# Sums of squares of the norms: VectorE folds three of four pairs of blocks before TensorE adds over features

## The chip, the cores and the metric

The kernel runs on one core of a Trainium2 chip. The metric is the device time of one execution in microseconds (us), lower is better. Five engines work side by side: PE (TensorE), DVE (VectorE), ACT (ScalarE), POOL (GpSimd) and SP (SyncE, which here issues the weight transfers). Semaphores alone tie them together.

## The reference

Two transformer blocks of depth 2 each, on one sequence of 256 tokens and 1024 features, in float32. What matters here are the norms over all 1024 features:

```python
def rms_norm(x, g):
    x32 = x.astype(jnp.float32)
    y = x32 * lax.rsqrt(jnp.mean(x32 * x32, axis=-1, keepdims=True) + EPS)
    return (y * g.astype(jnp.float32)).astype(x.dtype)
...
    for l in range(DEPTH):
        h = rms_norm(x, norm_mix_pre[l])
        proj = h @ w_in[l]
...
        x = x + rms_norm(merged @ w_out[l], norm_mix_post[l])

        h2 = rms_norm(x, norm_ffn_pre[l])
        gu = h2 @ w_ffn_in[l]
        f_g, f_u = jnp.split(gu, 2, axis=-1)
        f = (jax.nn.silu(f_g) * f_u) @ w_ffn_out[l]
        x = x + rms_norm(f, norm_ffn_post[l])
```

The second block has such a norm ahead of each of its six stages (mix, memory attention, feed-forward, and in the second layer a mixture of experts), and none behind them: the product is added to `x` as it is.

## The kernel before, in words

Everything lies with features on the 128 partitions and the 256 tokens along the free dimension. `x` is the tile `X`, eight feature blocks of 128 x 256, and is handled in four pairs of blocks (128 x 512), numbered 0 to 3. The program is ten stages in a row: mix and feed-forward of layer 0, the same of layer 1, then mix, memory and feed-forward of the second block, then mix, memory and experts. Each engine's program is one list of steps made in the same order (`steps`), and each engine picks its own kinds out of it, so an engine never passes a step of its own that still waits.

A product with a weight is made of three matmuls on a high and a low part of each operand (L1844, L1845, L1846; `wh` and `wl` are the parts of a weight unit of 128 x 1024). SP loads a unit, ACT copies its high part (L2315), DVE subtracts it for the low part (L2633). There are four slots for split units, so ACT starts the next unit when PE has freed a slot, and DVE follows ACT.

The sum of squares over 1024 features goes as follows. ACT squares a pair of blocks into one of six scratch tiles of `SC` (step `square`, L2330, or inside `y_out`, L2350). The step `sums` has PE multiply each 128 x 128 quarter of it, as the stationary operand, with a column of ones: four matmuls of one column per pair (L1849, written `ps<-CST,SC 128x1`), all 16 of a norm added up in one PSUM bank. The step `mean` has DVE make the inverse root of it in nine small instructions (L2642 and on, tile `RS`), and `spread` has PE copy it over the partitions (128x128 matmuls at L1849).

There are fourteen such norms of eight blocks: ten of `x` (one ahead of each stage; `x_sums`) and four of a stage's result (`ys`, in the mix and feed-forward stages of the first block). They differ in where the sums stand in the order:

- **Result norms** (four): `y_out` gives a square per pair, and the sums of pair n-1 are queued after pair n's product. The last two pairs come together behind the last product, in `residual_rms`, which then waits for the norm and adds it to `x`.
- **Heads** (five: the start of the program and behind each `residual_rms`): the next stage starts with `start`, in which PE multiplies the raw, not yet normed `x` with the first weights in parts of the features (`Wide.part`). Sums of pairs 0 and 1 stand behind the features of pairs 0 and 1, those of pairs 2 and 3 behind the features of pair 2, then `mean`, then the last part.
- **Added stages** (five: behind the stages of the second block): `added` (and a loop like it in `block2_mem`) takes each pair when the product is added to `X` (L2645 `X<-ps,X`), makes its parts (`x_parts` on ACT, L2335, and `x_low` on DVE, L2645 `b<-X,VEC,b`) and its square, and queues the sums of the pair before it. At most the last two pairs are left for `start`.

Two smaller norms (`mean_rs` over four blocks, or over the memory) use the same steps.

Of the kernel before, what the change touches and what calls it, by code (L numbers as in the profile page):

```python
# [175 lines left out]
def build(nc, ctx, ins, out):  # L176
# [205 lines left out]

    def sums(src, nt):
        o = Step("sums")
        o.src, o.nt, o.bk, o.wait, o.end = src, nt, a_bank(full=False), [], None
        return o

    def sums_pe(o, keep=0):
        while len(o.wait) > keep:
            sq = o.wait.pop(0)  # L390
            st = step("sums")
            st.o, st.sq = o, sq
            o.end = st.done = P.next("sums")
            sq.sc.out = st.done

# [7 lines left out]
    def mean_rs(src, nt, scale, eps, rdy, final=1.0, o=None):  # L403
        if o is None:
            o = sums(src, nt)
            for t0 in range(0, nt, 2):
                sums_pair(o, t0, rdy[t0 // 2] if nt == 8 and len(rdy) == 4 else rdy, keep=2)
                if t0 % 4 == 2 or t0 + 2 >= nt:
                    yield
                    sums_pe(o)  # L410
        sums_pe(o)
        st = mean(o, scale, eps, final)
        yield
        return spread(st)
# [645 lines left out]
    def added(g, keep=1):  # L1060

        for _ in g:
            while after:
                p = after.pop(0)
                xp = x_parts(p)
                x_squares(p)
                if p:
                    sums_pe(x_sums[0], keep)
                x_low(xp)
            yield  # L1070
# [768 lines left out]
    def pe_program(e):  # L1839
# [41 lines left out]
        def sums_step(st):  # L1881
# [4 lines left out]
            for u in range(2):  # L1886
                for b in range(2):
                    r = mm(o.bk.ps[:, b:b + 1], v[:, u, b * 128:(b + 1) * 128], ONES[:, 0:1], sq.t0 + u + b == 0, sq.t0 + u + b == o.nt)
            r.then_inc(st.done[0])
# [733 lines left out]
    def dve_program(e):  # L2623
# [54 lines left out]
        def split_step(st):  # L2678
# [4 lines left out]
            else:  # L2683
                stt(st.dst[1], st.src, st.fac, st.dst[0].bitcast(F32), MUL, SUB).then_inc(st.lo[0])

        def mean(st):
            o = st.o
# [635 lines left out]
        def tile_down(st):  # L3323
            if st.ending:
                for m, b in enumerate(st.bks):
# [6 lines left out]
                     up_gate=up_gate, up_gate_w=up_gate, up_rs=up_rs,  # L3332
                     mean=mean, hrs=hrs, scaled=scaled, residual=residual, kr_rope=kr_rope, glu=glu, conv=conv,
                     conv_mean=conv_mean, conv_z=conv_z, conv_y=conv_y, q_turn=q_turn, scores=scores, scores_pen=scores_pen, att_out=att_out, times=times,
# [233 lines left out]
```

## Time and profile before

| | us |
|---|---|
| median of 3 runs | 2828.19 |
| the runs | 2828.08, 2832.55, 2828.19 |
| the profiled execution's own time | 2826.45 |
| span of its instructions | 2824.7 |
| PE busy in the span | 2603.9 (92%) |
| DVE busy | 1949.6 (69%) |
| ACT busy | 1285.6 (46%) |

Mean granted TensorE clock 0.952. Times in the trace count from the first instruction. A matmul of the program in float32 leaves two records in the trace: `128x1 x8` of the program reads x16 there.

### The profile page before, as it was taken

To read this page: it belongs to the slowest core of one execution; us is meant where nothing else is said; L and a number is where in the kernel's file an instruction comes from. 1 tells how busy PE (TensorE), PEld (TensorE's weight loads), DVE (VectorE), ACT (ScalarE), POOL (GpSimd) and SP (SyncE) were. 2 spreads that over 40 slices of the span, in tenths; PEclk is the share of its full clock that TensorE was granted. 3 is DMA by queue.
4 is the path that set the end of the run, shared out by engine and by line. 5 is a ranking of instruction groups with operands and counts; after the bars stand their busy time and mean duration, and the time that the engine had idled before them with its cause. 6 is when DMAs were issued, how large, how long until landed. Compare 5 with 4: busy or idle time off the path is not lost.

```text
span 2824.7 us, 52188 instructions
## 1 busy us (share of the span) xinstructions
PE 2603.9 (92%) x20994; PEld 2423.6 (86%) x20994; DVE 1949.6 (69%) x3287; ACT 1285.6 (46%) x1939; POOL 350.5 (12%) x292
## 2 busy tenths in 40 slices
PE   7979889998799899899989999899888899999999
PEld 7879889988799899888878899888777888888887
DVE  5888767568887675676665676757565557566688
ACT  4445344444453444443333444343333447464576
POOL 0000000000000000000000000000000246455486
PEclk9999999999999999998989999989899799999999
DMA  5444445544444355342024355432032357576687
GB/s 197 155 142 150 142 134 182 181 162 153 140 147 150 130 185 179 122 142 76 18 75 150 120 186 177 156 120 76 17 103 95 131 180 251 199 234 223 199 304 263
DMA packets 135614, 433.90 MB, mean 154 GB/s; under 512 B 15408, under 2 KB 26032, under 8 KB 135120
## 3 DMA queue, kind: packets, MB, share of 16 engines
q1 hardware_dynamic: 94912, 286.25, 30.6%
q0 software_dynamic: 36512, 140.53, 14.7%
q10 hardware_dynamic: 3952, 3.79, 0.5%
q8 instruction: 169, 2.77, 0.4%
q14 instruction: 69, 0.57, 0.1%
HBM read 429.46 MB, written 1.05 MB: 152 GB/s over the span
## 4 chain that ended last, share of the span: by engine, by line
PE 73%; DVE 16%; ACT 5%; issue 4%; DMA 1%; POOL 0%; DVEq 0%; ACTq 0%; POOLq 0%
PE ps L1844 21%; PE ps L1846 20%; PE ps L1845 20%; PE ps L1849 12%; DVE wl L2633 4%; DVE b L2637 3%; DVE b L2645 2%; ACT wh L2315 2%; DVE SC L2645 1%; PE ps L1852 1%; DVE SC L2637 1%; DVE X L2637 0%; ACT SC L2394 0%; ACT b L2325 0%; DVE SC L2641 0%
## 5 line engine op out<-in xcount | busy, mean ns | idle before, releaser
L2633 DVE TENSOR_TENSOR wl<-wf,wh 128x1024 fp32r<-128x1024 f32 (+2 forms) x620 | 729.2, 1204 | 251.6 <-ACT wh L2315 246.8
L1844 PE MATMUL ps<-b,wh 128*128 128x256 f32 x2832 | 819.9, 289 | 89.6 <-DVE wl L2633 38.8
L1845 PE MATMUL ps<-b,wh 128*128 128x256 f32 x2832 | 807.4, 285 | 0.0
L1846 PE MATMUL ps<-b,wl 128*128 128x256 f32 x2832 | 806.1, 285 | 0.0
L2315 ACT ACTIVATE wh<-wf 128x1024 fp32r<-128x1024 f32 (+2 forms) x620 | 625.2, 1038 | 259.6 <-PE ps L1846 227.2
L1844 PEld LDWEIGHTS ps<-b,wh 128*128 128x128 f32 x2832 | 549.6, 194 | 101.2 <-issue 73.5
L1845 PEld LDWEIGHTS ps<-b,wh 128*128 128x128 f32 x2832 | 550.2, 194 | 0.2
L1846 PEld LDWEIGHTS ps<-b,wl 128*128 128x128 f32 x2832 | 549.2, 194 | 0.0
L1844 PE MATMUL ps<-HH,wh 128*128 128x256 f32 x1264 | 376.1, 298 | 37.9 <-DVE wl L2633 37.8
L1845 PE MATMUL ps<-HL,wh 128*128 128x256 f32 x1264 | 363.7, 288 | 0.0
L1846 PE MATMUL ps<-HH,wl 128*128 128x256 f32 x1264 | 363.4, 287 | 0.0
L1844 PEld LDWEIGHTS ps<-HH,wh 128*128 128x128 f32 x1264 | 248.7, 197 | 52.1 <-issue 50.9
L1845 PEld LDWEIGHTS ps<-HL,wh 128*128 128x128 f32 x1264 | 248.8, 197 | 1.9 <-issue 1.4
L1846 PEld LDWEIGHTS ps<-HH,wl 128*128 128x128 f32 x1264 | 248.5, 197 | 0.0
L1844 PE MATMUL ps<-wh,b 128*128 128x512 f32 (+2 forms) x560 | 218.1, 389 | 2.1 <-DVE wl L2633 1.3
L1845 PE MATMUL ps<-wl,b 128*128 128x512 f32 (+2 forms) x560 | 215.2, 384 | 0.0
L1846 PE MATMUL ps<-wh,b 128*128 128x512 f32 (+2 forms) x560 | 215.0, 384 | 0.0
L1849 PE MATMUL ps<-b,b 64*64 64x64 f32 (+5 forms) x3183 | 182.5, 250 | 25.6 <-DVE b L2637 13.4
L1849 PEld LDWEIGHTS ps<-b,b 64*64 64x64 f32 (+2 forms) x3183 | 161.8, 152 | 44.6 <-issue 16.1
L1849 PEld LDWEIGHTS ps<-CST,SC 128*128 128x128 f32 (+2 forms) x1140 | 130.5, 191 | 42.9 <-ACT SC L2363 19.0
L1849 PE MATMUL ps<-CST,SC 128*128 128x1 f32 (+4 forms) x1140 | 135.5, 270 | 33.4 <-DVE SC L2645 16.7
L2633 DVE TENSOR_TENSOR wl<-b,wh 128x1024 fp32r<-128x1024 f32 (+1 forms) x112 | 126.0, 1154 | 29.8 <-ACT wh L2315 29.3
(224 smaller groups left out, 3481.2 us busy)
## 6 DMA issues: line engine op xcount, KB each, us to landing
wf<-in_w_in_b SPq DMA_DIRECT2D x112, 512.0 KB, 4.1
wf<-in_w_in SPq DMA_DIRECT2D x80, 512.0 KB, 3.8
wf<-in_w_ffn_g SPq DMA_DIRECT2D x44, 512.0 KB, 3.5
wf<-in_w_ffn_u SPq DMA_DIRECT2D x44, 512.0 KB, 4.5
wf<-in_w_out SPq DMA_DIRECT2D x32, 512.0 KB, 3.5
wf<-in_w_ffn_out SPq DMA_DIRECT2D x32, 448.0 KB, 4.0
wf<-in_ffn_wg SPq DMA_DIRECT2D x22, 512.0 KB, 3.5
wf<-in_ffn_wu SPq DMA_DIRECT2D x22, 512.0 KB, 4.4
```

Source lines behind the costliest of these rows:

```text
L1844: e.matmul(o, stat[0], mov[0], start=first, stop=False)
L1845: e.matmul(o, stat[0], mov[1], start=False, stop=False)
L1846: return e.matmul(o, stat[1], mov[0], start=False, stop=end)
L1849: return e.matmul(o, l, r, start=first, stop=end)
L1852: return e.transpose(o, l, IDENT[0:l.shape[0], 0:l.shape[0]])
L2315: e.activation(u.whi, u.buf, ACT.Copy).then_inc(u.hi[0])
L2633: e.tensor_tensor(u.wlo, u.buf, u.whi.bitcast(F32), SUB).then_inc(u.lo[0])
L2637: return e.tensor_tensor(o, a, b, op)
L2645: return e.scalar_tensor_tensor(out=o, in0=a, scalar=s, in1=b, op0=op0, op1=op1)
```

## The change

The sums of pairs are no longer all made on PE. The first pair's square tile becomes a total; a new step `fold` has DVE add the squares of pair 1 and then of pair 2 to it in place (128 x 512 each). When pair 3 is taken, PE gets two steps one behind the other: the total, and pair 3. `mean_rs` keeps the old way. In `added` the step `x_low` moves ahead of the sums. ACT's program does not change.

```diff
+    def sums_part(o, sq, first, last):
+        st = step("sums")
+        st.o, st.sq, st.first, st.last = o, sq, first, last
+        o.end = st.done = P.next("sums")
+        sq.sc.out = st.done
 
     def sums_pe(o, keep=0):
         while len(o.wait) > keep:
             sq = o.wait.pop(0)
-            st = step("sums")
-            st.o, st.sq = o, sq
-            o.end = st.done = P.next("sums")
-            sq.sc.out = st.done
+            n = o.seen
+            o.seen += 1
+            if not o.fold:
+                sums_part(o, sq, n == 0, n == o.nt // 2 - 1)
+            elif n == 0:
+                o.total = sq
+            elif n < 3:
+                st = step("fold")
+                st.sc, st.sq, st.before = o.total.sc, sq, o.total.done
+                st.done = sq.sc.out = P.next("fold")
+                o.total = st
+            else:
+                sums_part(o, o.total, True, False)
+                sums_part(o, sq, False, True)
...
                 xp = x_parts(p)
                 x_squares(p)
+                x_low(xp)
                 if p:
                     sums_pe(x_sums[0], keep)
-                x_low(xp)
             yield
...
+        def fold(st):
+            E.wait_ge(st.before)
+            E.wait_ge(st.sq.done)
+            tt(st.sc.v, st.sc.v, st.sq.sc.v, ADD).then_inc(st.done[0])
```

PE, in the head of the first feed-forward stage (behind the features of pair 1; `b_13312` and `b_15360` are the high and low part of x). Before:

```order
L1844 MATMUL ps<-b_13312_128,wh 128x256
L1845 MATMUL ps<-b_15360_129,wh 128x256
L1846 MATMUL ps<-b_13312_128,wl 128x256
L1849 MATMUL ps<-CST,SC 128x1 x8
L1844 MATMUL ps<-b_13312_128,wh 128x256
```

The change, at the same products:

```order
L1861 MATMUL ps<-b_13312_128,wh 128x256
L1862 MATMUL ps<-b_15360_129,wh 128x256
L1863 MATMUL ps<-b_13312_128,wl 128x256
L1861 MATMUL ps<-b_13312_128,wh 128x256
L1862 MATMUL ps<-b_15360_129,wh 128x256
```

The eight sums of pairs 0 and 1 are gone, and the eight behind the features of pair 2 stay, now of the total and pair 3. (All lines behind the diff's first edit move by 17.)

DVE, at the end of the first mix stage: the last splits of weights, then the inverse root of the result norm. Before:

```order
L2645 SCALAR_TENSOR_TENSOR SC<-b_0_106,ps 128x512
L2637 TENSOR_TENSOR b_11264_130<-b_11264_130,SC 128x512
L2637 TENSOR_TENSOR b_15360_132<-b_11264_130,b_13312_131 128x512
L2633 TENSOR_TENSOR wl<-wf,wh 128x1024 x9
L2642 TENSOR_SCALAR RS<-ps 128x2
L2642 TENSOR_SCALAR RS<-RS 128x2
```

The change:

```order
L2654 TENSOR_TENSOR b_15360_132<-b_11264_130,b_13312_131 128x512
L2650 TENSOR_TENSOR wl<-wf,wh 128x1024 x6
L2654 TENSOR_TENSOR SC<-SC 128x512
L2650 TENSOR_TENSOR wl<-wf,wh 128x1024 x3
L2654 TENSOR_TENSOR SC<-SC 128x512
L2659 TENSOR_SCALAR RS<-ps 128x2
```

One fold stands between the splits and the second behind the last of them. In the head that follows, both folds stand behind the last split, right ahead of the inverse root.

DVE, at the end of the second block's first memory stage (`X<-ps,X` adds a pair; `b_15360_228` is the low part of the new x). Before:

```order
L2645 SCALAR_TENSOR_TENSOR X<-ps,X 128x512
L2645 SCALAR_TENSOR_TENSOR b_15360_228<-X,VEC,b_13312_227 128x256 x2
L2633 TENSOR_TENSOR wl<-wf,wh 128x1024 x2
L2645 SCALAR_TENSOR_TENSOR X<-ps,X 128x512
L2645 SCALAR_TENSOR_TENSOR b_15360_228<-X,VEC,b_13312_227 128x256 x2
L2633 TENSOR_TENSOR wl<-wf,wh 128x1024
L2642 TENSOR_SCALAR RS<-ps 128x2
```

The change:

```order
L2662 SCALAR_TENSOR_TENSOR X<-ps,X 128x512
L2662 SCALAR_TENSOR_TENSOR b_15360_228<-X,VEC,b_13312_227 128x256 x2
L2654 TENSOR_TENSOR SC<-SC 128x512
L2650 TENSOR_TENSOR wl<-wf,wh 128x1024 x2
L2662 SCALAR_TENSOR_TENSOR X<-ps,X 128x512
L2662 SCALAR_TENSOR_TENSOR b_15360_228<-X,VEC,b_13312_227 128x256 x2
L2654 TENSOR_TENSOR SC<-SC 128x512
L2650 TENSOR_TENSOR wl<-wf,wh 128x1024
L2659 TENSOR_SCALAR RS<-ps 128x2
```

Each fold stands between a pair's low part and the next split of weights.

## Rows read from the trace of the kernel before

**Rows 1.** The page: busy time, and the chain that ended last.

```profile
PE 2603.9 (92%) x20994; PEld 2423.6 (86%) x20994; DVE 1949.6 (69%) x3287; ACT 1285.6 (46%) x1939; POOL 350.5 (12%) x292
...
PE 73%; DVE 16%; ACT 5%; issue 4%; DMA 1%; POOL 0%; DVEq 0%; ACTq 0%; POOLq 0%
```

**Rows 2.** Timeline of PE: start, us, what; eight sums in a head.

```profile
386.03 1.84 PE L1849 MATMUL ps<-CST,SC 128*128 128x1 f32 x16
...
387.73 0.36 PE L1844 MATMUL ps<-b,wh 128*128 128x256 f32 x1
387.94 0.28 PE L1845 MATMUL ps<-b,wh 128*128 128x256 f32 x1
388.05 0.28 PE L1846 MATMUL ps<-b,wl 128*128 128x256 f32 x1
```

**Rows 3.** Timeline of PE: four sums behind a product of the first feed-forward.

```profile
542.93 0.95 PE L1849 MATMUL ps<-CST,SC 128*128 128x1 f32 x8
543.74 0.36 PE L1844 MATMUL ps<-b,wh 128*128 128x256 f32 x1
```

**Rows 4.** Groups of instructions by form, DVE: nearest form to a fold.

```profile
L2637 DVE TENSOR_TENSOR X<-X,SC 128x512 f32<-128x512 f32 x16 | 11.1, 692 | 0.6
```

**Rows 5.** Timeline of DVE, the same head; idle before and releaser in brackets.

```profile
392.56 0.16 DVE L2642 TENSOR_SCALAR RS<-ps 128x2 f32<-128x2 f32 x1 [8.15 <-PE ps L1849]
```

**Rows 6.** Timeline, end of the first mix stage: PE, then DVE.

```profile
355.58 1.05 PE L1849 MATMUL ps<-CST,SC 128*128 128x1 f32 x8 [0.54 <-ACT SC L2350]
356.50 0.37 PE L1844 MATMUL ps<-b,wh 128*128 128x256 f32 x1
...
368.68 1.90 PE L1849 MATMUL ps<-CST,SC 128*128 128x1 f32 x16
...
354.13 2.36 DVE L2633 TENSOR_TENSOR wl<-wf,wh 128x1024 fp32r<-128x1024 f32 x2 [6.89 <-ACT wh L2315]
...
367.24 1.23 DVE L2633 TENSOR_TENSOR wl<-wf,wh 128x1024 fp32r<-128x1024 f32 x1 [0.18 <-ACT wh L2315]
```

**Rows 7.** Timeline, end of the first feed-forward: PE, DVE, ACT.

```profile
575.66 1.98 PE L1849 MATMUL ps<-CST,SC 128*128 128x1 f32 x16
...
574.56 1.23 DVE L2633 TENSOR_TENSOR wl<-wf,wh 128x1024 fp32r<-128x1024 f32 x1 [1.57 <-ACT wh L2315]
...
575.94 0.60 ACT L2350 ACTIVATE SC<-ps 128x512 f32<-128x512 f32 x1 [1.41 <-PE ps L1846]
```

**Rows 8.** Timeline of PE and DVE: splits of weights that PE waits for.

```profile
1505.27 2.36 DVE L2633 TENSOR_TENSOR wl<-wf,wh 128x1024 fp32r<-128x1024 f32 x2 [0.98 <-ACT wh L2315]
...
1118.40 0.55 PE L1844 MATMUL ps<-b,wh 128*128 128x256 f32 x1 [2.99 <-DVE wl L2633]
...
1589.98 0.36 PE L1844 MATMUL ps<-b,wh 128*128 128x256 f32 x1 [0.19 <-DVE wl L2633]
...
2146.01 0.55 PE L1844 MATMUL ps<-HH,wh 128*128 128x256 f32 x1 [2.99 <-DVE wl L2633]
```

**Rows 9.** Timeline of DVE, end of the first memory stage.

```profile
1575.81 0.68 DVE L2645 SCALAR_TENSOR_TENSOR X<-ps,X 128x512 f32<-128x512 f32 x1
...
1580.08 0.68 DVE L2645 SCALAR_TENSOR_TENSOR X<-ps,X 128x512 f32<-128x512 f32 x1
...
1583.20 2.36 DVE L2633 TENSOR_TENSOR wl<-wf,wh 128x1024 fp32r<-128x1024 f32 x2 [0.98 <-ACT wh L2315]
1585.48 0.68 DVE L2645 SCALAR_TENSOR_TENSOR X<-ps,X 128x512 f32<-128x512 f32 x1
...
1588.61 1.23 DVE L2633 TENSOR_TENSOR wl<-wf,wh 128x1024 fp32r<-128x1024 f32 x1 [0.99 <-ACT wh L2315]
```

**Rows 10.** Timeline of PE: the last four sums, ahead of the experts.

```profile
2219.72 1.03 PE L1849 MATMUL ps<-CST,SC 128*128 128x1 f32 x8
```

**Rows 11.** Stretches: busy us of PE, PEld, DVE, ACT, POOL; granted clock; DMA.

```profile
1118.40:1121.70 3.30, 3.30 (x15) 3.30 (x16) 2.99 (x3) 1.36 (x2) 0.00 (x0) 0.50 0.72 196
...
1738.00:1792.00 54.00, 54.00 (x462) 53.85 (x461) 27.59 (x40) 20.83 (x27) 0.12 (x1) 1.00 0.51 164
```

More of the change, by code:

```diff
@@ L381, in split, with sums @@
         return [st.hi, st.lo]
-    def sums(src, nt):
+    def sums(src, nt, fold=True):
         o = Step("sums")
         o.src, o.nt, o.bk, o.wait, o.end = src, nt, a_bank(full=False), [], None
+        o.seen, o.total, o.fold = 0, None, fold
         return o
+    def sums_part(o, sq, first, last):
[3 more added lines that the diff above has]
+        sq.sc.out = st.done
     def sums_pe(o, keep=0):
@@ L404, in mean_rs @@
         if o is None:
-            o = sums(src, nt)
+            o = sums(src, nt, False)
             for t0 in range(0, nt, 2):
@@ L1887, in sums_step @@
                 for b in range(2):
-                    r = mm(o.bk.ps[:, b:b + 1], v[:, u, b * 128:(b + 1) * 128], ONES[:, 0:1], sq.t0 + u + b == 0, sq.t0 + u + b == o.nt)
+                    r = mm(o.bk.ps[:, b:b + 1], v[:, u, b * 128:(b + 1) * 128], ONES[:, 0:1], st.first and u + b == 0, st.last and u + b == 2)
             r.then_inc(st.done[0])
@@ L3332, in dve_program @@
                      up_gate=up_gate, up_gate_w=up_gate, up_rs=up_rs,
-                     mean=mean, hrs=hrs, scaled=scaled, residual=residual, kr_rope=kr_rope, glu=glu, conv=conv,
+                     fold=fold, mean=mean, hrs=hrs, scaled=scaled, residual=residual, kr_rope=kr_rope, glu=glu, conv=conv,
                      conv_mean=conv_mean, conv_z=conv_z, conv_y=conv_y, q_turn=q_turn, scores=scores, scores_pen=scores_pen, att_out=att_out, times=times,
```

## The prediction

> **What bounds the kernel now.** I began with the page. PE is busy for 2603.9 of 2824.7 us and holds 73% of the chain of work that ended last, DVE is busy for 1949.6 us and holds 16% [rows 1]. So work taken from PE is worth its time where PE runs without a pause, and work given to DVE is free where DVE waits for PE. That is a question for each of the fourteen norms, and the timeline around each answers it. I then read, place by place, when PE starts the sums, what it runs next, where it waits and for whom, and when DVE is free there.
>
> **The price of a sum.** In the head of the first feed-forward the eight matmuls of a group (16 records) start at 386.03 and the next product at 387.73: 1.70 us, 0.106 us a record [rows 2]. The first product behind them also takes 0.21 to the next start (387.73 to 387.94) where the next takes 0.11 (to 388.05), so leaving such a group saves about 0.08 more: 1.78 for eight, and with 0.81 for four (542.93 to 543.74) [rows 3] 0.89 for four.
>
> A rule speaks against this price. The Trainium skill, "TensorE: Matmul & The Clock Gate", section "Back-to-back issue gap", says that matmuls of few columns are bounded by an issue floor of about 25 ns. The 224 records removed would by that be worth an estimated 5.6 us and the time would be about 2823. The rows have 106 ns a record, four times the floor, and the same page's section on LDWEIGHTS gives the reason, an estimated 107 ns for 128 columns of a stationary operand: a sum with one column moves nothing, but loads 128 columns of squares. The trace decides, and I price by it.
>
> **The price of a fold.** No fold is in the trace. The nearest rows are adds of two SBUF tiles of 128 x 512 in float32, 0.692 us each over 16 instructions, in place as the fold is [rows 4]. I take 0.69. The 28 folds make 19.4 us of DVE time at most, and nothing at least.
>
> **Five heads.** DVE waits 8.15 us for PE, from the end of its last split at 384.41 to the inverse root at 392.56 [rows 5]. The squares are done by then, so both folds (1.4 us) are ready at about 385.8, more than 3 us before PE can reach the total. PE loses one group of eight: 1.78 us, and all that follows starts from the sums' end. If DVE's pause were not there the folds would cost 1.4. 5 x 1.78 = **8.9 us**.
>
> **Two mix results.** Ahead of the first product of pair 2 PE waits 0.54 us for the square of pair 0, then does the four sums, and starts the product at 356.50. Without them it could start at 355.0 or a little before, but its weight's low part is ready only at about 355.4 (the first of the two splits that start at 354.13) [rows 6]. So 1.1 is saved, and 0.89 at the next group. At the end the second fold stands behind the last split, which ends at 368.47 (367.24 + 1.23), 0.2 before PE's sums begin at 368.68 [rows 6]. Its high part comes from ACT, which makes a square and its copies just before and moves up only by the first saving and a part of the second, so the split then ends with PE's last product, and PE's lead of 1.99 shrinks by 0.1 and by the fold's 0.73. Net 1.1 us each: **2.2 us**.
>
> **Two feed-forward results.** Two groups of four go. Behind the last product DVE's last split ends at 575.79, so the second fold ends at 576.5. Before, PE did the sums of pair 2 from 575.66 on, while ACT made the last square (575.94 to 576.54) [rows 7]; now it waits for the fold and does all eight after it, 0.81 later. In layer 0 this leaves 2 x 0.89 - 0.81 = 0.97. In layer 1 the first group's gain vanishes, since PE waits 2.99 us for a split a little later, behind the rope tables, whose chain starts from the product and not from the sums [rows 8]. That leaves 0.08. Together **1.05 us**.
>
> **Five added stages.** Before, four sums after pairs 0, 1 and 2, and four (or eight) in the head. Here the last group grows from four to eight where three groups went.
> - First mix stage of the second block (sums of pair 3 already came with pair 2's): the first group's gain falls to a wait for a split that ends at 1506.5, and the second holds: 0.89 [rows 8].
> - First memory stage: DVE and ACT drive it. Add (0.68), parts, square, high part, low part, next add go round in 4.3 to 5.4 us whatever PE does, and the split that PE needs last ends at 1589.84, where PE already waits for it [rows 8, 9]. All three groups' gain is lost, and the final group, now eight, costs 0.81 on the path. The folds themselves fit: 0.69 in the 0.98 that DVE waits between a low part and a split; without that pause each would cost 0.69. Net -0.81.
> - Feed-forward: PE runs without a pause, 54.00 of 54.00 us [rows 11]; 3 x 0.89 - 0.81 = 1.86.
> - Second mix stage: both gains end in the wait of 2.99 at 2146.01, behind a transfer issued when x is ready [rows 8], and x is made by the DVE and ACT loop: 0.
> - Second memory stage: three groups of four go from a PE that runs nearly through, the last, which stood at 2219.72 right ahead of the inverse root, grows and waits a little for a fold behind pair 3's add [rows 10]: about 0.6, chosen between -0.8 and 1.9.
>
> Together **2.5 us**. The moved `x_low` costs nothing: it only keeps the fold out from ahead of a low part.
>
> **Sum.** 8.9 + 2.2 + 1.05 + 2.5 = 14.7 us. From the profiled execution's own 2826.45 that gives 2811.8. The three runs shown have a median 1.7 higher, 2828.19, and against it I predict **2813.5**.
>
> **The rivals.**
> - *Everything PE drops counts.* Of the 112 matmuls, five groups of eight at 1.78 and eighteen of four at 0.89 make 24.9 us: 2803.3. For it: PE's 92%. Against it: the waits just listed. Chance 0.06.
> - *The mixing stages swallow their share.* Long stretches behind the heads of the mix stages run through DVE and ACT chains. If these, and not the sums' end, set the next stage's start, only the two feed-forward heads (3.6) and the feed-forward results (1.05) keep their gain: -4.6, 2823.6, within the bound of 0.2%. Against it: each such chain begins with the inverse root, which waited for the sums [rows 5]. Chance 0.14.
> - *The loads of squares are hidden.* If a sum held PE for next to nothing beside the products, no place would gain, and the new waits for folds would stay, 0.73 behind each mix result and 0.81 behind each feed-forward result: +3.1, 2831.3, also within 0.2%. The page's issue floor is a rule of this kind. Against it: the next product starts 1.70 us later, not at once [rows 2]. Chance 0.03.
> - *The clock turns it into a loss.* Behind a wait of 2.99 us the granted clock is 0.50 for the next stretch (1.2 in place of 2.4 GHz) [rows 8, 11]. There 15 product records fill 3.3 us, 0.22 each; at 54.00 us for 462 records, 0.117 each, they would take 1.8, so that stretch gives away about 1.5 us. The change adds waits of PE: under 1 us behind four result norms, and two of 1 to 2 us in the first memory stage. If each of the fourteen norms brought one more such stretch, 14 x 1.5 = 21 us would go, and the time would be 2834.5. It decides from ten such stretches (no gain left), and can be told from fourteen. Against it: most places get denser, not looser. Chance 0.07.
>
> **How the numbers follow.** What I forecast has 0.70: gains of 9 to 20 us, 2808 to 2819, since how each stretch of low clock falls against the shifted work moves the sum by some microseconds. 0.2% of the time, 5.7 us, is about what can be told from no change. Faster then has 0.70 + 0.06 = 0.76, the same 0.14 + 0.03 = 0.17, slower 0.07. The range leaves out the loss and the outer part of the full gain and takes in the second rival: 2806 to 2825.
>
> **What would show it.** The page after has 224 fewer PE records and 28 more of DVE, the folds as `SC<-SC` of 128 x 512 at 0.69. In the heads PE goes through the features of pair 2 with no sums ahead, and DVE's wait before the inverse root shrinks from 8.15 to about 5. Behind the feed-forward results PE has a new wait of about 0.8 for `DVE SC`. In the first memory stage PE waits longer for splits and the end comes 0.8 later. The forecast is wrong if the folds take much longer than 0.69, if low splits or DVE loops move later by them, or if the mean granted clock falls clearly below 0.952.

## The result, and the profile after

| | before | changed |
|---|---|---|
| median, us | 2828.14 (4 runs) | 2805.15 (4 runs) |
| the runs, us | 2825.18 to 2832.55 | 2801.92, 2802.37, 2807.93, 2808.29 |
| profiled execution, us | 2826.45 | 2801.92 |
| span, us; mean granted clock | 2824.7; 0.952 | 2800.1; 0.955 |

The ratio is 0.9916, with a 95% interval from 0.9904 to 0.9929: 23 us faster. I had predicted 2813.5, 14.7 us faster, with a range down to 2806. The sign was right; the size lies just outside. Two later measurements of the same kernel, below, gave 0.9936 and 0.9945, which is about 2810 and 2813 us when put against the same 2828.14.

The page of the changed kernel, its head and the busy times:

```profile
span 2800.1 us, 51799 instructions
...
PE 2573.4 (92%) x20770; PEld 2394.1 (85%) x20770; DVE 1967.8 (70%) x3315; ACT 1284.7 (46%) x1939; POOL 348.6 (12%) x292
```

Against [rows 1] PE has 224 records fewer and DVE 28 instructions more, and PE's busy time fell by 30.5 us where DVE's grew by 18.2. In the groups of instructions by form, DVE, the folds have a row of their own:

```profile
L2654 DVE TENSOR_TENSOR SC<-SC 128x512 f32<-128x512 f32 x28 | 19.2, 686 | 0.2
```

686 ns each, against the 692 of [rows 4] by which I priced them, and DVE waited 0.2 us for them in all.

The head of the first feed-forward, timeline of PE, then of DVE (start, us, what, in brackets the idle time before and its releaser):

```profile
388.90 1.84 PE L1866 MATMUL ps<-CST,SC 128*128 128x1 f32 x16
390.61 0.36 PE L1861 MATMUL ps<-b,wh 128*128 128x256 f32 x1
...
383.21 1.23 DVE L2650 TENSOR_TENSOR wl<-wf,wh 128x1024 fp32r<-128x1024 f32 x1 [0.46 <-ACT wh L2332]
384.35 1.41 DVE L2654 TENSOR_TENSOR SC<-SC 128x512 f32<-128x512 f32 x2
390.78 0.16 DVE L2659 TENSOR_SCALAR RS<-ps 128x2 f32<-128x2 f32 x1 [5.02 <-PE ps L1866]
```

Both folds stand in DVE's pause and end 3 us before PE reaches the total. DVE's wait went from 8.15 us [rows 5] to 5.02, and the group that is left still takes 1.71 (388.90 to 390.61), as in [rows 2].

The end of the first mix stage (PE), and of the first feed-forward (PE, then DVE):

```profile
356.35 0.36 PE L1861 MATMUL ps<-b,wh 128*128 128x256 f32 x1 [0.46 <-DVE wl L2650]
368.69 1.95 PE L1866 MATMUL ps<-CST,SC 128*128 128x1 f32 x16 [0.90 <-DVE SC L2654]
```

```profile
572.82 1.95 PE L1866 MATMUL ps<-CST,SC 128*128 128x1 f32 x16 [0.63 <-DVE SC L2654]
...
570.93 1.22 DVE L2650 TENSOR_TENSOR wl<-wf,wh 128x1024 fp32r<-128x1024 f32 x1 [1.58 <-ACT wh L2332]
572.08 0.69 DVE L2654 TENSOR_TENSOR SC<-SC 128x512 f32<-128x512 f32 x1
```

These are the new waits that I had put there: for the weight's low part at 356.35, and for the last fold at 368.69 and 572.82, 0.63 to 0.90 us.

The end of the first memory stage, timeline of DVE:

```profile
1571.42 0.68 DVE L2662 SCALAR_TENSOR_TENSOR X<-ps,X 128x512 f32<-128x512 f32 x1
1572.68 0.89 DVE L2662 SCALAR_TENSOR_TENSOR b<-X,VEC,b 128x256 fp32r<-128x256 f32 x2 [0.58 <-ACT b L2352]
1573.49 0.68 DVE L2654 TENSOR_TENSOR SC<-SC 128x512 f32<-128x512 f32 x1
1574.55 1.23 DVE L2650 TENSOR_TENSOR wl<-wf,wh 128x1024 fp32r<-128x1024 f32 x1 [0.38 <-ACT wh L2332]
```

The fold sits in the pause ahead of the split, of which 0.38 of the 0.99 in [rows 9] is left. So it is free.

**Where the time came from.** The inverse root of a norm on DVE (`RS<-ps`) stands in both programs at the same place, so the distance from one such start to the next measures what lies between. The table has it for the two profiles above, and then the medians over eight profiles with sums of one column (before, changed three times, and four kernels with parts of the edit, all from the experiments below): those that lack the edit at the place (three or four) and those that have it there (four or five).

| what ends there, us | before | changed | median without | median with | difference | forecast |
|---|---|---|---|---|---|---|
| four heads behind results, each | 21.93 to 21.99 | 19.83 to 20.15 | 21.93 to 21.99 | 20.09 to 20.14 | -1.84 | -1.78 |
| mix result, layer 0 | 83.21 | 81.00 | 82.03 | 81.01 | -1.0 | -1.1 |
| mix result, layer 1 | 81.70 | 80.87 | 81.70 | 80.88 | -0.8 | -1.1 |
| first feed-forward result | 185.18 | 184.08 | 184.23 | 183.58 | -0.7 | -0.97 |
| second feed-forward result | 189.92 | 189.00 | 189.26 | 189.01 | -0.2 | -0.08 |
| added: first mix of block two | 62.21 | 61.38 | 62.26 | 61.38 | -0.9 | -0.89 |
| added: first memory stage | 54.89 | 54.68 | 53.63 | 54.68 | +1.0 | +0.81 |
| added: feed-forward | 192.85 | 191.21 | 192.61 | 190.69 | -1.9 | -1.86 |
| the head behind it and 50 us more | 72.13 | 71.02 | 72.75 | 71.38 | -1.4 | 0 |
| added: second mix | 80.86 | 80.92 | 80.95 | 81.06 | +0.1 | 0 |
| added: second memory stage | 54.73 | 49.60 | 54.65 | 51.05 | -3.6 | -0.6 |

The program's own start is not in it: PE's first product starts 1.53 us later in the profile after, and the first inverse root 0.28 earlier, so that head gained 1.8 like the rest. With five heads at 1.84 the differences sum to -18.6 us, where the forecast has -14.7. Two places make up what it lacks, and at both the granted clock differs.

The sum is not a full account, because the table has only the places of the edit. Right behind the program's first head, from the inverse root at 73.72 to the one at 287.40, the gain was lost again (before, then changed; us, busy us of PE, PEld, DVE, ACT, POOL, granted clock, DMA):

```profile
73.72:287.40 213.68, 190.47 (x1394) 176.80 (x1393) 181.39 (x335) 98.34 (x157) 0.00 (x0) 0.96 0.45 146
73.44:289.67 216.23, 193.06 (x1394) 179.26 (x1393) 181.75 (x335) 98.44 (x157) 0.00 (x0) 0.94 0.45 144
```

It is the same 1394 records, with PE busy for 2.6 us more at a lower clock: 23.9 us at half speed in place of 17.1. The five kernels with one-column sums that fold this head need 215.9 to 216.8 us here, the three that don't 213.7 to 215.3. From PE's first product to the inverse root that ends the stretch, before has 273.2 us and the changed kernel's three profiles 273.9, 273.4 and 274.7, so the fifth head brought nothing that lasts. Without it the table comes to -16.8. The places left out also differ between profiles of one kernel: from the last inverse root to the end the changed kernel took 599.9, 608.0 and 609.8 us. So the agreement of -18.6 with a measured 19 is partly chance.

Two rows need a second look. In the first memory stage before has 6.8 us at half clock and the kernels with and without the fold mostly 3.4; among those with 3.4 the fold costs 1.0 to 1.3 (54.7 against 53.5 and 53.6), while before and changed themselves differ by -0.2. The first feed-forward ran at one of two paces (last section). At equal pace its result norm gained 1.1: 185.18 against 184.08 and 183.99, and 184.2 against 183.05, 183.06 and 183.58.

### The profile page after: what moved, and what is told of

It reads as the page before. It is cut to its first block, busy times and chain, and to the rows that moved or that the text cites. A ratio compares the mean times of both kernels' runs of the same rounds, so it can differ in the third digit from the quotient of the medians.

```text
span 2800.1 us, 51799 instructions
## 1 busy us (share of the span) xinstructions
PE 2573.4 (92%) x20770; PEld 2394.1 (85%) x20770; DVE 1967.8 (70%) x3315; ACT 1284.7 (46%) x1939; POOL 348.6 (12%) x292
## 4 chain that ended last, share of the span: by engine, by line
PE 44%; DVE 9%; ACT 3%; issue 3%; DMA 1%; POOL 0%; DVEq 0%; ACTq 0%; POOLq 0%
PE ps L1861 11%; PE ps L1862 11%; PE ps L1863 11%; PE ps L1866 9%; DVE b L2654 2%; DVE wl L2650 2%; ACT wh L2332 1%; DVE b L2662 1%; PE ps L1869 1%; DVE SC L2662 1%; DMA b<-in_moe_down,b 0%; DVE b L3221 0%; ACT SC L2420 0%; ACT b L2342 0%; DVE S L3220 0%
## 5 line engine op out<-in xcount | busy, mean ns | idle before, releaser
L1866 PEld LDWEIGHTS ps<-b,b 64*64 64x64 f32 (+2 forms) x3183 | 160.5, 151 | 44.5 <-issue 15.6
L1866 PEld LDWEIGHTS ps<-CST,SC 128*128 128x128 f32 (+1 forms) x916 | 103.7, 192 | 44.9 <-ACT SC L2380 18.9
L1866 PE MATMUL ps<-CST,SC 128*128 128x1 f32 (+3 forms) x916 | 109.1, 278 | 35.3 <-DVE SC L2662 16.7
```

The costliest lines, as they stand in the source:

```text
L1866: return e.matmul(o, l, r, start=first, stop=end)
```

## Experiments

All changes are against the kernel named. Each ratio is against the kernel before on the same chip, with its 95% interval; the changed kernel's 0.9916 was measured with 4 runs.

"Low clock" stands for stretches in which the granted clock is 0.50 (1.2 in place of 2.4 GHz); the last such stretch of a profile is counted whole, though it ends up to 3 us behind the span. Three theories, stated before the first run. **A**: the forecast's terms hold, and besides the sums with one column let the granted clock fall, so that taking them out gives clock back. **B**: the terms hold, and the rest is how the stretches of low clock happened to fall in a few runs. **C**: each matmul that PE drops counts in full (24.9 us).

### The fold in the result norms alone

Changed kernel, with

```diff
-            x_sums[0] = sums(x3, 8)
+            x_sums[0] = sums(x3, 8, False)
```

> The fold is made for the four result norms alone; the ten norms of x have their four groups of sums as before (the moved low part of the added stages stays moved). Direct terms as forecast: two mix results at 1.1, feed-forward results at 0.97 and 0.08, together 3.2 us, so about 2825. Theory A (the forecast's terms hold, and on top of them the sums with one column let the granted clock fall, so that taking them out gives clock back): up to 2 us more, 2823 to 2825. Theory B (terms hold, and the rest of the 23 us is how the stretches of low clock happened to fall): 2825 with 3 us to either side. Theory C (every matmul that PE drops counts in full, nothing is hidden): 8 groups of four at 0.89, 7.1 us, 2821.

Measured: 2826.35 us (12 runs), ratio 1.0005 (0.9994 to 1.0017), that is +1.4 us, with -1.7 to +4.8 in the interval. No gain in the whole, where 3.2 was expected. Its profile does show the gains in place (80.86 and 80.96 us at the two mix results), and it gives them back in the stretches up to 2166 us of before, where PE's low clock added up to 15.7 and 11.6 us against 10.2 and 3.4, at places that the edit does not touch. Theory C (7.1 us) falls. Against A and B it says little, except that a term of 3 us does not show in a median.

### The fold in the five heads alone

```diff
-            x_sums[0] = sums(x3, 8)
+            x_sums[0] = sums(x3, 8, stage_no[0] < 5)
...
-        yd, ys = [], sums(Y, 8)
+        yd, ys = [], sums(Y, 8, False)
```

> The fold is made for the five norms of x whose squares come ahead of a stage's start (the program's start and behind the four result norms); results and added stages have their sums as before. Direct term as forecast: 5 x 1.78 = 8.9 us, about 2819. Theory A: in these heads PE runs without a wait on either side of the sums, so clock comes back only a little, 1 to 3 us more: 2816 to 2818. Theory B: 2819 with 3 us to either side. Theory C: 2819 as well. The trace is to show the eight sums ahead of the last part gone and DVE's wait before the inverse root down from 8.15 to about 5.

(The second part of the edit stands twice in the kernel, once for mix and once for feed-forward results; so it does in the next experiment.)

Measured: 2815.74 us (9 runs), ratio 0.9971 (0.9959 to 0.9983): -8.2 us, as the term says (8.9), though an interval of 3.4 to either side does not tell five heads that keep their gain (9.2) from four (7.4). DVE's wait before the inverse root:

```profile
392.26 0.16 DVE L2659 TENSOR_SCALAR RS<-ps 128x2 f32<-128x2 f32 x1 [4.98 <-PE ps L1866]
```

The heads measure 20.09, 20.09, 20.09 and 20.15 us against 21.94, 21.96, 21.93 and 21.99. No more clock came back here than without the edit: 10.24 us of low clock behind each start of such a head in both kernels.

### The fold in the five added stages alone

```diff
-            x_sums[0] = sums(x3, 8)
+            x_sums[0] = sums(x3, 8, stage_no[0] > 4)
...
-        yd, ys = [], sums(Y, 8)
+        yd, ys = [], sums(Y, 8, False)
```

> The fold is made for the five norms of x that added stages make; heads behind results, and the results, have their sums as before. Direct terms as forecast: 2.5 us, about 2825.5. Theory A: most of what the forecast missed lies here, above all in the second memory stage, where sums stood between waits of PE: 5 to 7 us more, 2819 to 2821, with a low stretch fewer between 2195 and 2235 and a higher mean granted clock than before has. Theory B: 2825.5 with 3 us to either side. Theory C: ten groups of four at 0.89, 8.9 us, 2819.

Measured: 2820.60 us (12 runs), ratio 0.9991 (0.9980 to 1.0002): -2.5 us, the forecast's term, and the interval leaves out the 5 to 7 more of theory A and the 8.9 of C. (The plain medians, 2820.60 and 2824.52, differ by 3.9.) Its one profiled execution was 10 us below that median. In it the second memory stage takes 49.81 us against 54.73, with the low stretches behind its sums gone. So A's place is right; its size in the whole is not borne out by this kernel.

### Sums of 128 columns, nothing folded

Kernel before, with

```diff
-                    r = mm(o.bk.ps[:, b:b + 1], v[:, u, b * 128:(b + 1) * 128], ONES[:, 0:1], sq.t0 + u + b == 0, sq.t0 + u + b == o.nt)
+                    r = mm(o.bk.ps[:, b * 128:(b + 1) * 128], v[:, u, b * 128:(b + 1) * 128], ONES, sq.t0 + u + b == 0, sq.t0 + u + b == o.nt)
...
-            rsqrt(st.sc.v[:, 2:4], o.bk.ps[:, 0:2], st.scale, st.eps, 2, st.rs, final=st.final, out=o.bk.out)
+            rsqrt(st.sc.v[:, 2:4], o.bk.ps[:, 0:256].rearrange("p (b n) -> p b n", n=128)[:, :, 0], st.scale, st.eps, 2, st.rs, final=st.final, out=o.bk.out)
```

and the same for `mean_moe`.

> The kernel before, with all its sums, but each sum multiplies by 128 columns of ones in place of one, into 256 columns of the bank, of which the mean reads columns 0 and 128. The same 448 records and the same loads of squares; each record now also moves 128 columns, which by the rows of 128 columns costs about what the load costs, so the price of a group may stay near 1.70 or grow by at most 0.8 us in all where it does not overlap. Theory A (a sum of one column counts as idle for the granted clock): the clock rises, 4 to 8 us are gained, 2820 to 2824, mean clock about 0.955. Theory B and theory C: no gain, 2828 or some us more, mean clock 0.952.

Measured: 2822.77 us (12 runs), ratio 0.9987 (0.9975 to 0.9998): -3.7 us, with -7.1 to -0.6 in the interval. More work on PE, and if anything less time. In the heads the low clock behind the first norm shrinks. The same 13.8 us from the inverse root on (stretches: busy us of PE, PEld, DVE, ACT, POOL, granted clock, DMA), before:

```profile
370.60:384.40 13.80, 7.46 (x40) 6.73 (x40) 11.18 (x26) 6.56 (x13) 0.00 (x0) 0.63 0.09 37
```

and with 128 columns:

```profile
371.70:385.50 13.80, 7.48 (x43) 6.88 (x44) 11.18 (x26) 6.56 (x13) 0.00 (x0) 0.75 0.11 44
```

Half speed lasts 10.24 us behind the first inverse root of all four such heads before, and 6.83 here in three of the four (10.24 in the head of the layer-1 mix stage), and in the second memory stage one of two low stretches is gone (51.77 us against 54.73). What PE did ahead of the stretch is the same but for the sums' columns. That is what theory A expects, at a size of 3 to 4 us in the whole.

This does not hang on one profile. Of the 36 such heads in the nine profiles with one-column sums (the doubled kernel left out) 35 have 10.2 us of low clock; of the 16 in the four profiles with 128 columns 14 have 6.8. And over all runs the mean granted clock was 0.954 to 0.959 here (median 0.957, 12 runs), against 0.949 to 0.954 in 30 of 31 runs of the kernel before beside it (median 0.952). So theory B alone cannot hold: the clock follows the edit of the sums. By the two medians that is an estimated 28 us less at half speed, worth at most 14 us (0.005 x 2 x 2825, and half of it), while the time fell by 3.7.

### The changed kernel again

> The changed kernel once more, in more runs than the 4 behind the result, beside the kernel before on the same chip. Theory A (the terms of the forecast, 14.7 us, and on top of them granted clock that the one-column sums had cost, some 8 us in every run): ratio 0.991 to 0.993 again. Theory B (the terms, and for the rest how the stretches of low clock happened to fall in the few runs of either kernel; runs of the kernel before alone went from 2818.6 to 2834.1 us in the experiments on the parts): ratio 0.9935 to 0.996. The parts folded alone gave +1.4 - 8.2 - 2.5 = -9.3 us together, with some 5 us of uncertainty, which speaks for B.

Measured: 2807.49 us (5 runs), ratio 0.9936 (0.9921 to 0.9952), -18 us. That is the edge of B's figures (0.9935 to 0.996), and the interval takes in A's upper one (0.993) too, so it decides nothing. It does not fit the three parts, though: alone they gave +1.4, -8.2 and -2.5, together -9.3 us with some 6 to either side, half of what they give in one kernel. No run here explains that.

### All four pairs folded

Changed kernel, with

```diff
-            elif n < 3:
+            elif n < 3 or o.fold == 4:
...
                 o.total = st
+                if n == 3:
+                    sums_part(o, st, True, True)
             else:
...
-            x_sums[0] = sums(x3, 8)
+            x_sums[0] = sums(x3, 8, 4)
```

> The changed kernel, but in the ten norms of x VectorE also adds the squares of the fourth pair, so that TensorE sums one tile in place of two (four matmuls in place of eight); the four result norms stay as in the changed kernel. By the terms: in the heads of a start the folds still end well ahead of the sums, 5 x 0.89 = 4.4 us gained; in the added stages' norms PE's last group shrinks by 0.81 but waits 0.7 longer for a fold where the inverse root follows at once (second memory stage), about 3 us gained in the other four. Together 6 to 8 us below the changed kernel, -21 to -23 us against before by theory B, -29 to -31 by theory A.

Measured: 2808.63 us (6 runs), ratio 0.9936 (0.9917 to 0.9954), the same as the changed kernel beside it, where 6 to 8 us less was expected. The heads gained what was expected (19.19 to 19.27 us against 20.1). The profile lost as much elsewhere: 1.2 us in the step behind the first mix of block two (13.84 for 12.64, 6.8 us of low clock for 3.4), and 2.8 in the experts, where PE waited 7.7 us for nothing that the profile shows, 4.6 of it at once (the changed kernel beside it has 3.6 of this kind):

```profile
PE ps L1868 <- issue: 7.7, 5, 4.6
```

### The changed kernel with sums of 128 columns

The edit of the kernel with 128 columns, made in the changed kernel.

> The changed kernel with sums of 128 columns in place of one (columns 0 and 128 are read). Theory A: few one-column records are left, so little clock is left to gain: 0 to 3 us below the changed kernel. Theory B: no difference from it, within 3 us.

Measured: 2807.24 us (5 runs), ratio 0.9932 (0.9919 to 0.9944), within 2 us of the changed kernel beside it. Its profile has 238.0 us of low clock against 266.3, and the heads measure 19.7 us for 20.1. Both theories allow the time. The granted clock was 0.955 to 0.958 in its runs and 0.952 to 0.956 in the changed kernel's, again higher with 128 columns.

### Every sum made twice

Kernel before, with

```diff
-            for u in range(2):
-                for b in range(2):
-                    r = mm(o.bk.ps[:, b:b + 1], v[:, u, b * 128:(b + 1) * 128], ONES[:, 0:1], sq.t0 + u + b == 0, sq.t0 + u + b == o.nt)
+            for c in (2, 0):
+                for u in range(2):
+                    for b in range(2):
+                        r = mm(o.bk.ps[:, c + b:c + b + 1], v[:, u, b * 128:(b + 1) * 128], ONES[:, 0:1], c == 2 and sq.t0 + u + b == 0, c == 0 and sq.t0 + u + b == o.nt)
```

> The kernel before with every group of sums made twice, the second time into two columns that nobody reads: 224 matmuls more (448 records) with their loads. By the price of the rows: five heads of eight (1.70 each, two pairs of which had been summed in stages before, so more lies in the results and added stages), at most 56 groups of four at 0.81 = 45 us, less what hides in waits of PE (about a third of the added stages' and results' groups): 30 to 40 us slower than before. Theory A: twice as many one-column records also cost as much clock as the first ones, 8 us more or above: 40 to 50 us slower, mean clock at 0.948 or below. Theory B: 30 to 40 us, mean clock about as before's or above, since the added work runs at full clock.

Measured: 2928.75 us (5 runs), ratio 1.0365 (1.0350 to 1.0379): 100.6 us slower by the means of the runs. My count was wrong: the page has 576 records more (21570 against 20994), not 448, since norms inside the mixing stages use the same step. At 0.106 each they make 61 us. The rest goes with 79.1 us more of low clock (353.8 against 274.8; the 351.6 in the next expectation is 2.2 too low), mean clock 0.940. Groups of 32 records now stand in the heads. Timeline of PE, and below it two stretches of low clock:

```profile
397.91 3.63 PE L1849 MATMUL ps<-CST,SC 128*128 128x1 f32 x32
...
405.84 4.04 PE L1849 MATMUL ps<-CST,SC 128*128 128x1 f32 x32
```

```profile
402.05:405.46 3.41, 3.41 (x18) 3.41 (x17) 0.00 (x0) 0.00 (x0) 0.00 (x0) 0.50 0.00 0
408.88:415.71 6.83, 6.83 (x35) 6.83 (x34) 3.90 (x11) 2.12 (x2) 0.00 (x0) 0.50 0.13 20
```

PE is busy without a pause on both sides of these groups. The clock falls to half 0.5 us behind the first group and 3.0 us into the second (which is why that one lasts 4.04). Before, with groups of 16 at the same places, it was 1.00 from 381 to 579 us.

### Every sum made twice, with 128 columns

The same doubling, and each sum with 128 columns of ones.

> As x1_twice (every group of sums made twice, the second time where nobody reads), but all sums multiply by 128 columns of ones. x1_twice was 100.6 us slower: its 576 records more (the doubled groups are not only those of the fourteen norms, but also those of norms inside the mixing stages, which the expectation of x1_twice left out) make 576 x 0.106 = 61 us, and its stretches of low clock grew from 274.7 to 351.6 us, which at half speed is worth up to 38 us. Theory A (records with one column let the granted clock fall): the clock's part goes, 576 x 0.112 = 64 us and at most 10 more, 60 to 80 us slower than before, low clock below 300 us in all. Theory B (low stretches follow waits and the work's place in time, not columns): 95 to 110 us slower, low clock again about 350 us.

Measured: 2878.64 us (4 runs), ratio 1.0175 (1.0154 to 1.0197): 49.8 us slower, half of the other's loss, with as many instructions and more columns. Low clock 241.4 us in all, less than before's, mean clock 0.959. The same places, timeline of PE and stretches:

```profile
398.00 3.73 PE L1849 MATMUL ps<-CST,SC 128*128 128x128 f32 x32
...
404.38 3.73 PE L1849 MATMUL ps<-CST,SC 128*128 128x128 f32 x32
```

```profile
402.10:405.50 3.40, 3.40 (x32) 3.40 (x32) 0.00 (x0) 0.00 (x0) 0.00 (x0) 1.00 0.00 0
408.50:415.30 6.80, 6.78 (x58) 6.62 (x57) 6.16 (x17) 3.56 (x6) 0.00 (x0) 1.00 0.36 120
```

A group takes as long as with one column (3.73 against 3.63), so the columns do not set its price, and the clock stays at 1.00. This separates A from B, which expected about 350 us of low clock with 128 columns as well. The time lies below both expectations' ranges (60 to 80 for A), since the low clock fell even below before's.

### No fold in the second memory stage

Changed kernel, with

```diff
-            x_sums[0] = sums(x3, 8)
+            x_sums[0] = sums(x3, 8, stage_no[0] != 9)
```

> The changed kernel with the fold left out in one norm, that of the second memory stage, where four groups of four are summed again. From the inverse root at the end of its first norm to that of its last (54.73 us before; 49.60, 52.29 and 49.81 in the kernels with the fold, of which the 52.29 has a low stretch of its own 17 us in), theory A: 53 to 55 us, with low stretches right behind the first and second group of sums, as in all four kernels that had one-column sums there, and the whole 3.5 to 5 us slower than the changed kernel. Theory B: the direct price alone, 0.6 us by the forecast or 1.8 by two groups that count in full: 50.5 to 52 us in that stretch.

Measured: 2815.88 us (6 runs), ratio 0.9950 (0.9934 to 0.9966), 2.5 us slower than the changed kernel beside it, which intervals of some 4 us do not tell from nothing. The stage itself answers better: 54.57 us, as theory A says, against 52.40 of the changed kernel beside it. Timeline of PE, and the stretch behind the second group:

```profile
2190.28 0.95 PE L1866 MATMUL ps<-CST,SC 128*128 128x1 f32 x8
...
2195.34 0.95 PE L1866 MATMUL ps<-CST,SC 128*128 128x1 f32 x8
```

```profile
2198.77:2205.60 6.83, 6.78 (x32) 6.79 (x33) 0.00 (x0) 1.68 (x3) 0.00 (x0) 0.50 0.01 2
```

The same place before has the groups at 2200.59 and 2207.14, and the clock down twice:

```profile
2203.79:2207.20 3.41, 3.41 (x19) 3.41 (x18) 0.63 (x2) 0.63 (x2) 0.00 (x0) 0.50 0.00 0
2210.62:2217.45 6.83, 6.80 (x32) 6.80 (x33) 0.00 (x0) 1.66 (x3) 0.00 (x0) 0.50 0.00 0
```

And in the changed kernel's first profile, at the same distance from the stage's norm:

```profile
2188.30:2191.70 3.40, 3.32 (x30) 3.18 (x29) 2.81 (x6) 2.16 (x6) 0.00 (x0) 1.00 0.01 2
2195.10:2198.60 3.50, 3.35 (x32) 3.26 (x30) 1.89 (x4) 1.43 (x3) 0.00 (x0) 1.00 0.02 5
```

30 and 32 records fit where 19 and (in twice the time) 32 did. A low stretch behind the first group, which theory A wanted too, did not come in this kernel (the clock was 1.00 from 2178.3 to 2198.7). The clock is not all the sums' doing, either. The later two profiles of the changed kernel, 52.29 and 52.40 us, have a low stretch of 3.41 us at this second place too, without sums ahead of it, and one of 6.83 well before the edit's place, which costs 1.43 us (28.45 for 27.03 us from the stage's norm to the same product). This kernel has that early one as well, and at the second place 6.83 where they have 3.41: 2.2 us longer, for the sums and 3.4 us of low clock more.

### A candidate below both

From the changed kernel: all pairs folded in the heads, none in the first memory stage's norm, three elsewhere, and sums of 128 columns.

```diff
-            x_sums[0] = sums(x3, 8)
+            x_sums[0] = sums(x3, 8, 4 if stage_no[0] < 5 else stage_no[0] != 6)
```

with the edits of the kernels with four pairs and with 128 columns.

> A candidate below both: the changed kernel with all four pairs folded in the heads of a start (one group of four sums left), no fold in the first memory stage's norm, three pairs folded elsewhere, and sums of 128 columns. Against the changed kernel: five heads at 0.9 (19.2 against 20.1 us in the profiles) = -4.5, the first memory stage -1.1, and by theory A -1.5 to -3 for the columns: 7 to 8 us below it, -27 us or ratio 0.990 to 0.991 against before. Theory B: -5.6 below the changed kernel, ratio 0.991.

Measured: 2805.50 us (5 runs, 2803.28 to 2806.60), ratio 0.9911 (0.9896 to 0.9925), and 8 us below the changed kernel beside it (2813.42), whose interval does not touch this one's. Its profile shows each part: heads 18.79 to 18.86 us (20.1), first memory stage 53.55 (54.4 to 54.7), second memory stage 49.10 with no low clock (52.4). It has the lowest ratio here, as expected, though its interval takes in the 0.9916 first measured for the changed kernel. Its granted clock was 0.956 to 0.958, the changed kernel's beside it 0.949 to 0.954.

### The changed kernel a third time

> The changed kernel again, beside b1_best and n9_not_mem1 on one chip. The two measurements so far were 0.9916 and 0.9936 of the kernel before. If the terms and the clock's part in the second memory stage (3.5 us more than forecast) are all there is, 18 to 20 us below before, ratio 0.9930 to 0.9936; if the first measurement's 23 us hold in general, 0.9916. From the inverse root at the second memory stage's first norm to its last: 49.6 to 52.3 us.

Measured: 2813.42 us (6 runs, 2811.46 to 2819.83), ratio 0.9945 (0.9930 to 0.9959), -15.6 us, second memory stage 52.40 us. The changed kernel has now 0.9916, 0.9936 and 0.9945, on average 0.9932 or 19 us.

## Why the prediction was right and where it failed

- **The price of a sum and of a fold**: right. 0.106 us a record and 1.84 us for a group of eight with its switch (forecast 1.78), 686 ns for a fold (690).
- **Five heads**: right, 1.84 for 1.78 each, 9.2 us in all for 8.9, and -8.2 when done alone. What failed is that the program's first head keeps its gain: the stretch behind it ran 3.4 to 6.8 us longer at half clock and took 2.2 to 3.1 us back, so some 7.4 lasted. This is the loss that the rival on the clock feared, at one place.
- **Two mix results**: 1.8 us for 2.2, with the waits where they were put (0.90 for the fold where 0.73 was priced).
- **Two feed-forward results**: 0.7 and 0.2 for 0.97 and 0.08; between profiles that ran the first feed-forward's products at the same pace the first is 1.1.
- **Added stages**: right for the first mix (-0.9), the first memory stage (+1.0 for +0.81, its sign too), the feed-forward (-1.9) and the second mix (0).
- **Second memory stage**: this is the term that failed most. "About 0.6, chosen between -0.8 and 1.9" measured 3.6 (3.3 by means). I had priced the groups that go and a wait for the fold, all at the clock of before. The fold itself is worth about 0.9: 51.77 us with sums of 128 columns and no fold against 52.29 - 1.43 = 50.86 with it, both with 3.41 us of low clock ahead of the last sums. The other 2.4 to 2.7 us are clock, which the prediction's term put at nothing. With one-column groups the stage runs 6.8 to 13.7 us at half clock (five profiles), with 128 columns 3.4 (two). Folded, up to its last group of sums, it has none, or 3.4 beside the early stretch that the edit can't reach; folded with 128 columns none (two profiles, 49.10 us each). In the profiled pair of the first measurement the stage fell from 54.73 to 49.60, 5.1 us.
- **"How each stretch of low clock falls against the shifted work moves the sum by some microseconds"**: true, but I let it go to both sides of zero alike and gave a rival's chance only to a loss. Of the 72 us behind the feed-forward of block two, all profiles with the edit in the added stages run 10.2 to 13.7 us at half clock, and all with one-column sums and no fold there 17.1, worth 1.4 us. With 128 columns and no fold it is 17.1 in one kernel and 13.7 in the doubled one, so the columns do not settle it. That the work stands elsewhere against the low stretches is what I would argue; it was not shown.
- **The first measurement**: the remaining 4 us of its 23 did not come back in two more. The profiled pair differs by 24.5 us, 9.8 more than forecast: 4.5 of it are the second memory stage, 1.1 the 72 us just named, and 4.0 the experts, which the edit does not touch (596.66 us from the last inverse root to the last `X<-ps,X`, against 600.67 before, with 10.7 us less of low clock); the rest about cancels. In the later two profiles they took 604.71 and 606.50. There PE waited, in the second profile of the changed kernel (what PE waited for in the experts: total, times, longest):

```profile
PE ps L1861 <- issue: 3.6, 2, 3.1
PE ps L1866 <- ACT b L2598: 1.9, 1, 1.9
```

and in the first profile

```profile
PE ps L1861 <- DVE wl L2650: 1.3, 1, 1.3
PE ps L1866 <- ACT b L2598: 1.1, 1, 1.1
```

  What the 3.1 us were spent on the profile does not show. They do not come from the edit: all eight profiles of these two later chips have such waits, the two kernels without any fold (every sum made twice) too, with 607 to 608 us from the last inverse root to the end of the span, while before and the changed kernel have none in the first measurement. So these waits would lengthen both sides of a later ratio, and do not by themselves explain why it is nearer to 1.

So the prediction's 14.7 stands against 19 on average. The step that failed is the pricing of each norm at the clock of before: for the second memory stage it gave 0.6 where 3.6 was measured, for the 72 us behind the feed-forward nothing where 1.4 was, and for the program's first head 1.78 where nothing lasted. That the three misses leave the whole within a few us of the forecast is luck in part.

Of the rivals, "everything PE drops counts" gave 24.9, close to the first measurement, and for the wrong reason: its terms for the results, the first memory stage and the second mix are refuted place by place, and the fold in the results alone brought nothing that a median shows. "The loads of squares are hidden" falls with the doubled sums. "The clock turns it into a loss" had the clock's sign wrong for the whole: the mean granted clock of the profiles rose from 0.952 to between 0.953 and 0.955. One new low stretch of 3.41 us did appear where PE now waits for splits in the first memory stage (1570.60), as that rival feared, in two of the changed kernel's three profiles; it is in the 54.68 us there, and the 6.83 us that before has earlier in this stage are gone.

What stays open: why three measurements of one pair of kernels differ by more than their intervals (0.9916 and 0.9945), why the fold in the results alone, whose places each gain, measured +1.4 us, why the parts sum to half of the whole, and why the clock fell more often behind the program's first head.

## What to carry to other kernels

Matmuls with a whole stationary load and one moving column cost PE's time for the load and may cost clock behind them; where they can't be folded away on an engine that waits anyway, wider ones of the same duration can be the better choice. Price a fold place by place: it is worth its full time only where PE runs through and the adding engine is idle before PE needs the total, and nothing where a split or a transfer is what PE waits for next. And below some 5 us, compare distances between the same two instructions over several profiles rather than medians of the whole, and include the stretches that the edit does not touch: a gain can be lost again behind its place, as it was behind the first head.

## What the runs showed of the hardware that was not expected

- The granted clock fell around busy work too: with two groups of 32 records of one column, PE busy on both sides, it was 0.50 for 3.41 and 6.83 us; with 128 columns at the same places, 1.00. Over the kernel that made 353.8 against 241.4 us of low clock and some 50 us of time.
- A matmul record of 128 x 128 float32 takes as long with one column as with 128: groups of 32 at full clock took 3.63 and 3.73 us.
- Products ran at one of two paces, at full clock, in different executions. From 410 to 510 us, before and one of the changed kernel's later profiles (before, the changed kernel's first profile and the fold in the results have 851 or 852, five others of one-column sums 859 or 860):

```profile
410.00:510.00 100.00, 100.00 (x851) 100.00 (x850) 77.54 (x124) 48.75 (x71) 0.00 (x0) 1.00 0.56 183
```

```profile
410.00:510.00 100.00, 100.00 (x859) 100.00 (x859) 78.48 (x128) 47.20 (x70) 0.00 (x0) 1.00 0.60 187
```

  0.9% more records in the same time. It explains a whole microsecond in the first feed-forward, on both sides of the edit; its cause is open.
- One stretch of 51 us behind the second block's feed-forward took 50.9 or 47.9 us (10.2 or 3.4 us of low clock), in kernels with and without the edit alike.
